# Larger weight transfers over more of the expert loop of a mixture-of-experts decoder layer

## The chip, the cores and the metric

One NeuronCore of a Trainium2 chip (trn2) runs the whole layer. The metric is device time in microseconds (us) of one execution. All data are float32.

## What is computed

One decoder layer over 256 tokens of width 1024: a mixer (a matrix-memory group and an attention group side by side), then a mixture of 32 experts of which each token takes 4, then a gate with per-layer embeddings. The expert part holds nearly all of the bytes: each expert has an up matrix of 1024 x 2048 (8 MB) and a down matrix of 1024 x 1024 (4 MB), so 32 experts are 384 MB that are read once.

```python
logits = (t @ w_router + b_router)
top_vals, top_idx = lax.top_k(logits, TOP_K)
wts = jax.nn.softmax(top_vals, axis=-1)
...
for e in range(N_EXPERTS):
    hu = t @ w_gu[e] + b_gu[e]
    glu = jnp.minimum(hu[:, :D_FF], SWIGLU_LIMIT)
    lin = jnp.clip(hu[:, D_FF:], -SWIGLU_LIMIT, SWIGLU_LIMIT)
    act = glu * jax.nn.sigmoid(SWIGLU_ALPHA * glu) * (lin + 1.0)
    y = y + gates[:, e:e + 1] * (act @ w_dn[e] + b_dn[e])
```

## The kernel before

**Stages.** TensorE (PE) first computes the mixer, up to about 165 us of the trace, then the experts in 16 pairs (pair 0 to 15), then the last gate from about 1069 us on. Up to 64 tokens of each expert are gathered, multiplied with the expert's weights and scattered back; with these inputs one pass of the pair loop suffices.

**Positions.** Expert weights come in chunks of 2 MB (128 partitions x 4096 numbers): four for an expert's up matrix, two for its down matrix, so 12 a pair. `STREAM` gives their order within a pair: four up chunks of the even expert, two up chunks of the odd one, the even expert's two down chunks, the odd one's other two up chunks, its two down chunks. The last pair uses `LAST_STREAM`: all eight up chunks, then the four down chunks. The chunks of all pairs in this order are the positions 0 to 192 (`AT`); one of them, position 150 in pair 12, holds the embedding weights instead. Pair p (up to 12) begins at position 12 p, so pair 1 at 12, pair 2 at 24, pair 4 at 48; pair 15 begins at 181. Two more, 193 and 194, are the weights of the final gate.

**The ring.** A chunk lives in one of ten slots of 2 MB in SBUF (`ring`); an eleventh place, slot 10, is used once. `SLOT_OF[n]` is the slot of position n, picked by the loop at lines 100 to 109: the slot whose last occupant is the oldest. Positions with `FIRST_DOUBLE <= pair < END_DOUBLE` are planned two at a time: a pair of neighbouring slots (0 and 1, 2 and 3, ...) is filled by one transfer of 4 MB, and the pair is picked whose later occupant is the oldest. `FIRST_OF[n]` is the position at which the transfer that brings n begins.

**Loads and releases.** All weight loads are issued by SyncE (SP), in order of position, from one instruction stream. `refill` (line 554 on) waits on the counter `chunk_done` until PE has finished the occupant of the slot (`wait_released`), for a 4 MB transfer until it has finished the later of the two occupants; then `load_position` issues one DMA: line 539 for 2 MB, line 527 for 4 MB.

```python
elif m + 1 < POSITIONS and FIRST_OF[m + 1] == m:
    wait_released(sp, ps, max(occupant(m), occupant(m + 1)))
else:
    wait_released(sp, ps, occupant(m))
load_position(m)
```

PE takes the positions in the same order: `up_chunk` (16 matmuls of line 1129) and `down_chunk` (16 of line 1159) each begin with `wait_position`, which waits for the landing of the transfer that brought the position, so for both halves of a 4 MB one. Between them lie the gathers (line 1072), scatters (line 1080), transposes (1136, 1149) and biases (1121). The last positions, 189 to 192, are loaded and used in parts (lines 531 to 550).

Of the kernel before, what the change touches and what calls it, by code (L numbers as in the profile page):

```python
# [33 lines left out]
def hybrid_layer(nc, x, p, mix_norm_g, w_in, conv_w, conv_b, igate_b, fgate_b, mlstm_head_g, q_norm_g,  # L34
# [10 lines left out]
    PAIRS = E // 2  # L45
# [13 lines left out]
    PRE_SLOT = [4, 6, 8, 0, 1, 2, 4, 6, 8]  # L59
    MOE_SLOT = list(range(RING))  # L60
    HT_SLOT, CONST_SLOT, GATE_SLOT, V_SLOT, OUT_SLOT, MIX_SLOT = 3, 5, 6, 7, 8, 9
    FIRST_DOUBLE, END_DOUBLE = 4, 15
    LATE = 16 * 7
    GATE_STEPS = 10
    POST = 7
# [7 lines left out]
    POSITIONS = PER_PASS + 1  # L73
# [14 lines left out]
    AT = CHUNKS[:PLE_AT] + [None] + CHUNKS[PLE_AT:]  # L88
# [3 lines left out]
    def last_in(slot):  # L92

        return max(i for i, held in enumerate(SLOT_OF) if held == slot)

    def usable(slot):

        return slot != X_SLOT and (len(SLOT_OF) <= PLE_AT or slot != SLOT_OF[PLE_AT])

    while len(SLOT_OF) < POSITIONS + FINALS:  # L100
        n = len(SLOT_OF)
        if n < POSITIONS and AT[n] is not None and FIRST_DOUBLE <= AT[n][0] < END_DOUBLE:
            assert AT[n][:3] == AT[n + 1][:3] and AT[n][3] % 2 == 0 and AT[n + 1][3] == AT[n][3] + 1
            low = min((s for s in range(0, X_SLOT, 2) if usable(s) and usable(s + 1)), key=lambda s: max(last_in(s), last_in(s + 1)))
            SLOT_OF += [low, low + 1]
            FIRST_OF += [n, n]
        else:
            SLOT_OF.append(min((s for s in range(X_SLOT) if usable(s)), key=last_in))
            FIRST_OF.append(n)
# [2020 lines left out]
```

## Time and profile before

| | us |
|---|---|
| median of 3 runs | 1104.46 |
| lowest and highest of them | 1103.58, 1105.56 |
| the profiled execution, its own time | 1103.95 |
| its span in the trace | 1101.7 |
| PE busy, share of the span | 1072.8, 97% |
| bytes read from HBM | 430.04 MB, 391 GB/s over the span |

The span is what the trace covers; 2.3 us of the execution's time lie around it. A landing is the moment at which all 16 DMA engines have finished their part of a transfer. The profile gives it as the time from the issue on SP.

### The profile page before, as it was taken

What the parts mean: (1) busy time and instruction counts of PE and PEld (TensorE: products, weight loads), DVE (VectorE), ACT (ScalarE), POOL (GpSimd) and SP (SyncE); (2) the same over time, 40 slices, a digit from 0 to 9 for tenths busy, and PEclk for the clock granted to TensorE, in tenths of its full rate; (3) what the DMA queues carried; (4) which work ended last, traced back from release to release, by engine and by line L of the source; (5) the groups of instructions that cost most, each with busy time, mean ns of one, the idle gap of its engine ahead of it and who ended that gap; (6) DMA issues with size and microseconds to landing.
All of it is one profiled execution on the core that took longest, in us unless ns stands there. A gap on an engine that the chain in (4) does not pass through costs nothing.

```text
span 1101.7 us, 11963 instructions
## 1 busy us (share of the span) xinstructions
PE 1072.8 (97%) x5130; PEld 448.5 (41%) x5130; DVE 258.4 (23%) x531; ACT 144.6 (13%) x283; POOL 17.3 (2%) x45
## 2 busy tenths in 40 slices
PE   9999999999999999999998989898989899999998
PEld 5485563434343434343433333333333243534334
DVE  4274232231111212121211111121111011211122
ACT  4134341100000000000000000000000110000022
POOL 2001200000000000000000000000000000000000
PEclk9999999999999999999999999999999899999999
DMA  9943589999999999999999999999999999999981
GB/s 348 365 170 114 239 349 396 427 406 428 427 428 434 428 432 433 429 429 432 432 429 430 432 431 428 434 429 434 431 428 430 432 429 431 431 430 425 422 358 39
DMA packets 33787, 431.87 MB, mean 392 GB/s; under 512 B 5207, under 2 KB 5727, under 8 KB 16582
## 3 DMA queue, kind: packets, MB, share of 16 engines
q1 hardware_dynamic: 33520, 431.06, 92.9%
q8 instruction: 41, 0.67, 0.2%
q14 instruction: 12, 0.10, 0.0%
q10 hardware_dynamic: 214, 0.04, 0.0%
HBM read 430.04 MB, written 1.06 MB: 391 GB/s over the span
## 4 chain that ended last, share of the span: by engine, by line
PE 78%; DMA 21%; DVE 0%; issue 0%; ACT 0%; DVEq 0%; ACTq 0%
PE hu L1129 29%; DMA ring<-in_w_gate_up 17%; PE po L1159 17%; PE aux L1072 5%; PE hu L752 5%; PE aux L1080 3%; DMA ring<-in_w_down 3%; PE hu L758 3%; PE hu L1121 2%; PE hu L768 2%; PE po L1136 1%; PE hu L794 1%; PE aux L1340 1%; PE aux L1105 1%; PE hu L1159 1%; PE po L1340 1%
## 5 line engine op out<-in xcount | busy, mean ns | idle before, releaser
L1129 PE MATMUL hu<-ring,num_xg 128*64 128x512 f32 x1920 | 435.1, 600 | 16.8 <-DMA ring<-in_w_gate_up 16.6
L1129 PEld LDWEIGHTS hu<-ring,num_xg 128*64 128x64 f32 x1920 | 132.1, 137 | 299.8 <-issue 273.0
L1159 PE MATMUL po<-ring,arena 128*64 128x512 f32 x976 | 219.2, 601 | 6.2 <-DMA ring<-in_w_down 6.2
L1159 PEld LDWEIGHTS po<-ring,arena 128*64 128x64 f32 x976 | 70.4, 138 | 149.8 <-issue 146.4
L1711 DVE TENSOR_SCALAR arena<-hu 128x512 f32<-128x512 f32 x31 | 21.4, 692 | 426.0 <-PE hu L1129 426.0
L1687 DVE TENSOR_TENSOR arena<-arena,aux 128x512 f32<-128x512 f32 x58 | 37.3, 684 | 133.7 <-PE aux L1080 121.9
L1072 PEld LDWEIGHTS aux<-num_xg,big 128*128 128x128 f32 x512 | 58.4, 192 | 13.0 <-issue 13.0
L1072 PE MATMUL aux<-num_xg,big 128*128 128x128 f32 x512 | 61.4, 278 | 0.0
L752 PE MATMUL hu<-ring 128*128 128x512 f32 x128 | 56.7, 595 | 0.0
L1700 DVE TENSOR_SCALAR arena<-iota_s,posm,gates 128x128 f32<-128x128 f32 x64 | 17.9, 342 | 118.2 <-PE po L1159 115.3
L2034 ACT ACTIVATE hu<-arena 128x512 f32<-128x512 f32 x31 | 18.6, 601 | 194.4 <-DVE arena L1711 194.4
L2050 ACT COPY arena<-po 128x512 f32<-128x512 f32 x16 | 9.4, 585 | 223.2 <-PE po L1149 223.2
L1080 PE MATMUL aux<-num_xg,arena 64*128 64x512 f32 x124 | 35.0, 641 | 0.1
L752 PEld LDWEIGHTS hu<-ring 128*128 128x128 f32 x128 | 23.8, 190 | 27.7 <-issue 27.4
L1121 PE MATMUL hu<-bias,sel_part 32*64 32x512 f32 x256 | 34.8, 612 | 0.0
L1080 PE MATMUL aux<-arena 64*128 64x512 f32 x124 | 31.8, 589 | 0.0
L2042 ACT COPY num_xg<-po 128x512 f32<-128x512 f32 x16 | 9.4, 585 | 158.7 <-PE po L1159 158.7
L2038 ACT COPY arena<-po 128x512 f32<-128x512 f32 x31 | 18.1, 585 | 91.1 <-PE po L1136 91.1
L758 PE MATMUL hu<-ring 128*128 128x256 f32 x128 | 29.5, 385 | 0.0
L1129 PE MATMUL hu<-ring,arena 128*64 128x512 f32 x128 | 28.3, 595 | 0.1
L758 PEld LDWEIGHTS hu<-ring 128*128 128x128 f32 x128 | 23.7, 190 | 4.8 <-DVE ring L1490 1.0
L768 PE MATMUL hu<-ring 128*128 128x512 f32 (+1 forms) x64 | 25.5, 542 | 0.0
(275 smaller groups left out, 607.0 us busy)
## 6 DMA issues: line engine op xcount, KB each, us to landing
ring<-in_w_gate_up SPq DMA_DIRECT2D x44, 4096.0 KB, 35.3
ring<-in_w_down SPq DMA_DIRECT2D x22, 4096.0 KB, 35.7
ring<-in_w_gate_up SPq DMA_DIRECT2D x37, 2048.0 KB, 15.2
ring<-in_w_down SPq DMA_DIRECT2D x14, 2048.0 KB, 16.6
ring<-in_w_in SPq DMA_DIRECT2D x6, 2048.0 KB, 16.2
ring<-in_w_down SPq DMA_DIRECT2D x8, 1024.0 KB, 32.5
ring<-in_w_gate_up SPq DMA_DIRECT2D x6, 1024.0 KB, 7.0
ring<-in_w_out SPq DMA_DIRECT2D x2, 2048.0 KB, 11.3
```

Source lines behind the costliest of these rows:

```text
L752: last = mm(bank, hT[:, k, tt * P:(tt + 1) * P], slot(n, NB, K)[:, k, :], start=(k == 0), stop=(k == K - 1))
L758: last = mm(bank[:, 0:S], slot(n, NB, K)[:, k, ct * P:(ct + 1) * P], hT[:, k, :], start=(k == 0), stop=(k == K - 1))
L768: last = mm(bank[:, lo:hi], mixT[:, k, tt * P:(tt + 1) * P], slot(n, D, 4)[:, k % 4, b * NB + lo:b * NB + hi], start=(k == 4), stop=(k == 3))
L1072: last = mm(bank[:, (k % 4) * P:(k % 4 + 1) * P], h2[:, tt, k * P:(k + 1) * P], onehot[:, tt, :, :].rearrange("p e s -> p (e s)"), start=( ...
L1080: return mm(bank, ghotT[r, e, tt * P:(tt + 1) * P], out_s[e][r, :], start=(e == 0), stop=(e == 1 and not more))
L1121: mm(hu[n * SLOTS:(n + 1) * SLOTS, 2 * e + b, :], expert_rows(b, expert), features(bias[32 * b:32 * b + E, :], n), start=first, stop=False ...
L1129: last = mm(hu[n * SLOTS:(n + 1) * SLOTS, 2 * e + b, :], rows_of[:, k, e * SLOTS:(e + 1) * SLOTS], features(w[:, o:o + D], n), start=first ...
L1159: last = mm(bank[n * SLOTS:(n + 1) * SLOTS, :], actT[:, f, h * SLOTS:(h + 1) * SLOTS], w[:, o:o + NB], start=(h == 0 and f == 0), stop=(h ...
L1340: last = mm(fin_bank(q, lo, hi), x3T[:, k, tt * P:(tt + 1) * P], final_slot(k // 4, D, 4)[:, k % 4, n * NB + lo:n * NB + hi], start=(k == ...
L1687: v.tensor_tensor(quad(xt, q), quad(xt, q), banks[q], ALU.add).then_inc(y_done, 1)
L1711: v.tensor_scalar(glu, hu[:, 2 * e, :], LIMIT, None, ALU.min).then_inc(glu_ready, 1)
L2034: a.activation(hu[:, 2 * e, :], gated(2 * pair + e), ACT.Sigmoid, scale=ALPHA).then_inc(sig_ready, 1)
```

## The change

`FIRST_DOUBLE` is 2 instead of 4, `END_DOUBLE` goes, and of pair 15 the up chunks (kind 0) are planned two at a time as well. The down chunks of pair 15 stay single.

```diff
-    FIRST_DOUBLE, END_DOUBLE = 4, 15
+    FIRST_DOUBLE = 2
...
-        if n < POSITIONS and AT[n] is not None and FIRST_DOUBLE <= AT[n][0] < END_DOUBLE:
+        if n < POSITIONS and AT[n] is not None and FIRST_DOUBLE <= AT[n][0] and AT[n][:2] != (PAIRS - 1, 1):
             assert AT[n][:3] == AT[n + 1][:3] and AT[n][3] % 2 == 0 and AT[n + 1][3] == AT[n][3] + 1
             low = min((s for s in range(0, X_SLOT, 2) if usable(s) and usable(s + 1)), key=lambda s: max(last_in(s), last_in(s + 1)))
             SLOT_OF += [low, low + 1]
```

So 24 transfers of 2 MB in pairs 2 and 3 become 12 of 4 MB, and 8 in pair 15 become 4. The plan that the rule gives, for the places where a load's release changes (the number is the position that PE must have finished before the load is issued):

| load of | before: slot, waits for | after: slots, wait for |
|---|---|---|
| 24 / 25 | 3, 14 / 4, 15 | 4 and 5, 16 |
| 26 / 27 | 5, 16 / 6, 17 | 6 and 7, 18 |
| 28 / 29 | 7, 18 / 8, 19 | 8 and 9, 20 |
| 30 / 31 | 9, 20 / 0, 21 | 0 and 1, 22 |
| 46 / 47 | 5, 36 / 6, 37 | 6 and 7, 37 |
| 48 / 49 | 8 and 9, 40 | 8 and 9, 39 |
| 50 / 51 | 0 and 1, 42 | 0 and 1, 41 |
| 52 / 53 | 2 and 3, 44 | 2 and 3, 43 |
| 54 / 55 | 4 and 5, 46 | 4 and 5, 45 |
| 56 / 57 up to 179 / 180 | the same | the same |
| 181 / 182 | 1, 141 / 8, 173 | 8 and 9, 174 |
| 183 / 184 | 9, 174 / 2, 175 | 2 and 3, 176 |
| 185 / 186 | 3, 176 / 4, 177 | 4 and 5, 178 |
| 187 / 188 | 5, 178 / 6, 179 | 6 and 7, 180 |
| 189 | 7, 180 | 1, 141 |
| 193, 194 | 2, 184; 3, 185 | 3, 184; 4, 185 |

On SP, in pairs 1 and 2, the instruction stream before has these rows (line, what, shape, what it waits for, how many in a row). The first four rows are positions 13 to 23, the x6 row is 24 to 29 of pair 2, the last row its 30 and 31:

```order
L539 DMA ring<-in_w_gate_up 128x4096 [waits chunk_done] x5
L539 DMA ring<-in_w_down 128x4096 [waits chunk_done] x2
L539 DMA ring<-in_w_gate_up 128x4096 [waits chunk_done] x2
L539 DMA ring<-in_w_down 128x4096 [waits chunk_done] x2
L539 DMA ring<-in_w_gate_up 128x4096 [waits chunk_done] x6
L539 DMA ring<-in_w_down 128x4096 [waits chunk_done] x2
```

And now:

```order
L539 DMA ring<-in_w_gate_up 128x4096 [waits chunk_done] x5
L539 DMA ring<-in_w_down 128x4096 [waits chunk_done] x2
L539 DMA ring<-in_w_gate_up 128x4096 [waits chunk_done] x2
L539 DMA ring<-in_w_down 128x4096 [waits chunk_done] x2
L527 DMA ring<-in_w_gate_up 128x8192 [waits chunk_done] x3
L527 DMA ring<-in_w_down 128x8192 [waits chunk_done]
```

The six loads of positions 24 to 29 have become three of twice the size, the two of 30 and 31 one; nothing ahead of them moved.

On SP at the turn from pair 14 to pair 15, before (the first three rows are the last loads of pair 14, the x8 row the up chunks of pair 15):

```order
L527 DMA ring<-in_w_down 128x8192
L527 DMA ring<-in_w_gate_up 128x8192
L527 DMA ring<-in_w_down 128x8192
L539 DMA ring<-in_w_gate_up 128x4096 x8
L531 DMA ring<-in_w_down 128x2048
```

And now:

```order
L527 DMA ring<-in_w_down 128x8192
L527 DMA ring<-in_w_gate_up 128x8192
L527 DMA ring<-in_w_down 128x8192
L527 DMA ring<-in_w_gate_up 128x8192 x4
L531 DMA ring<-in_w_down 128x2048
```

Eight loads have become four; the down chunks behind them are loaded in the same parts as before. The matmuls of PE keep their order in all pairs; only what each waits for changes.

## Rows read from the trace of the kernel before

**Rows 1.** the page's slices of the span: GB/s in 40 slices of 27.5 us

```profile
GB/s 348 365 170 114 239 349 396 427 406 428 427 428 434 428 432 433 429 429 432 432 429 430 432 431 428 434 429 434 431 428 430 432 429 431 431 430 425 422 358 39
```

**Rows 2.** chain that ended last, in order of time: start us, us, what

```profile
340.72 7.02 PE hu L1129 x32
...
394.06 7.02 PE hu L1129 x32
...
542.89 38.94 DMA ring<-in_w_gate_up
...
1060.12 5.30 PE hu L1159 x24
1069.39 7.05 PE aux L1340 x16
```

**Rows 3.** busy time by stretch; the last three columns: PE clock, DMA share, GB/s

```profile
core 0: us, PE busy (x) PEld busy (x) DVE busy (x) ACT busy (x) POOL busy (x), PEclk, DMA share, GB/s
190.00:245.00 55.00, 54.92 (x280) 21.23 (x278) 16.15 (x27) 5.08 (x9) 0.00 (x0) 1.00 1.00 417
245.00:347.00 102.00, 102.00 (x514) 38.82 (x512) 21.13 (x38) 7.67 (x13) 0.00 (x0) 1.00 1.01 428
347.00:540.00 193.00, 193.00 (x972) 74.26 (x970) 37.07 (x65) 14.74 (x25) 0.00 (x0) 1.00 1.01 432
540.00:870.00 330.00, 306.96 (x1492) 113.02 (x1490) 60.01 (x108) 23.58 (x40) 0.00 (x0) 0.99 1.00 431
870.00:981.00 111.00, 111.00 (x539) 43.77 (x537) 20.59 (x38) 9.41 (x16) 0.00 (x0) 0.98 1.00 431
981.00:1045.00 64.00, 64.00 (x324) 23.92 (x322) 12.80 (x22) 5.31 (x9) 0.00 (x0) 1.00 1.00 425
```

**Rows 4.** timeline of PE in pair 1, positions 15, 16 and 18, 19: start us, us, what

```profile
233.98 7.09 PE L1129 MATMUL hu<-ring,num_xg 128*64 128x512 f32 x32
...
246.18 7.04 PE L1159 MATMUL po<-ring,arena 128*64 128x512 f32 x32
```

**Rows 5.** timeline of SP, its DMA issues, 215 to 260 us: start us, us, what

```profile
222.35 5.83 SPq L539 DMA_DIRECT2D ring<-in_w_down  x2
233.50 20.08 SPq L539 DMA_DIRECT2D ring<-in_w_gate_up  x6
```

**Rows 6.** line 539, the issue of position 23 and that of position 25, with landing

```profile
L539 SPq DMA_DIRECT2D ring<-in_w_down x1: 328/328/328, 227.9 to 227.9; - x1
...
DMA to landing us min/median/max: 9.4/9.4/9.4
...
L539 SPq DMA_DIRECT2D ring<-in_w_gate_up x1: 328/328/328, 237.7 to 237.7; - x1
...
DMA to landing us min/median/max: 11.2/11.2/11.2
```

**Rows 7.** DMA before an issue into an empty queue, and that issue's landing

```profile
100.00:106.50 6.50, 6.50 (x18) 2.63 (x16) 0.51 (x3) 2.10 (x3) 1.41 (x2) 1.00 0.00 0
...
L539 SPq DMA_DIRECT2D ring<-in_w_gate_up x1: 327/327/327, 106.5 to 106.5; - x1
...
DMA to landing us min/median/max: 7.1/7.1/7.1
```

**Rows 8.** timeline of PE in pair 15, positions 184, 185 and 186 to 188

```profile
1030.42 7.09 PE L1129 MATMUL hu<-ring,num_xg 128*64 128x512 f32 x32
...
1039.13 10.52 PE L1129 MATMUL hu<-ring,num_xg 128*64 128x512 f32 x48
```

**Rows 9.** line 539, the issue of position 186 and that of position 188, with landing

```profile
L539 SPq DMA_DIRECT2D ring<-in_w_gate_up x1: 328/328/328, 999.8 to 999.8; - x1
...
DMA to landing us min/median/max: 34.7/34.7/34.7
...
L539 SPq DMA_DIRECT2D ring<-in_w_gate_up x1: 328/328/328, 1012.1 to 1012.1; - x1
...
DMA to landing us min/median/max: 32.2/32.2/32.2
```

## The prediction

> **What bounds the kernel now.** I read the busy time by stretch first. TensorE (PE) is busy all the time in every stretch but the one from 540 to 870 us, where it stands for 330.00 - 306.96 = 23.0 us [rows 3]. That looks like a kernel bound by PE with a small hole. The last two columns of the same rows say otherwise: from 190 us on the DMA share is 1.00 and the rate 425 to 432 GB/s in every full stretch, and the page's slices show that it stays there up to some 30 us before the end [rows 1, 3]. Next the chain that ended last, for the pace of each. The same group of matmuls starts at 340.72 and at 394.06, so PE needs 53.3 us for a pair [rows 2]. A pair's weights are 12 x 2.097 MB = 25.2 MB, at 431 GB/s 58.4 us. DMA is thus 5 us a pair slower than PE; PE lives off its stock in the ring, which is used up at 543 us, where the chain goes over to DMA [rows 2]. **From 190 us on the last byte of the weights comes when the DMA engines have moved them all, and a microsecond in which they have nothing queued is given back nowhere**, whoever is waiting at that moment. PE has slack at 240 us, by the two paces some 303 / 53.3 x 5.1 = 29 us, and that slack does not help: to spend it sooner only brings the first stall forward.
>
> In the last pair the two are level. PE does not stand between 870 and 1045 us [rows 3], and from there its chain runs through to the final gate at 1069.39 [rows 2].
>
> **The change, part 1: the first load of pair 2 is issued later.** Here the ring is full and SP waits for PE. Before, position 24 (2 MB) is issued at 233.50, when PE is through with position 14 [rows 5]. Position 23, the last one ahead of it, is issued at 227.9 and lands 9.4 later, at 237.3 [rows 6]. So the queue is fed 3.8 us before it would run dry. Now 24 and 25 come in one transfer that needs slots 4 and 5, and so waits for position 16. PE is through with 15 and 16 at 233.98 + 7.09 = 241.1 [rows 4]. From 237.3 to 241.1 nothing is queued.
>
> What a start from an empty queue costs can be read where the trace has one. In 100 to 106.5 us the DMA share is 0.00, then a 2 MB load is issued at 106.5 and lands 7.1 us later [rows 7]. The second 2 MB of the new transfer follow at 431 GB/s, 4.9 us. It lands at 241.1 + 7.1 + 4.9 = 253.1. Before, position 25 was there at 237.7 + 11.2 = 248.9 [rows 6]. **Cost: +4.2 us.** It can't be less than with no start time at all, 241.1 + 9.7 = 250.8, which is +1.9. It can be more: before, 23 to 25 took 248.9 - 237.3 = 11.6 us, where the pace is 9.8 for 4 MB, though the queue was not empty, only short [rows 6]. If a short queue costs these 1.8 us, the next load may cost them again: 26 and 27 wait for position 18, which ends at 246.18 + 3.5 = 249.7 [rows 4], 3.4 us ahead of 253.1. So the bounds are +1.9 and +6.0, and I take +4.2, since both its parts are measured and 1.8 us in one place may be an accident of that place. The later loads of pairs 2 and 3 also wait for a position closer to their own, 8 or 9 back instead of 10, but each pair DMA falls 5 us further behind PE, so that slots come free well before DMA gets to them.
>
> **Part 2: the rate.** With 2 MB transfers the rate is 428 GB/s (245 to 347 us), with 4 MB transfers 431 and 432 [rows 3]. 4.194 MB take 9.80 us at 428 and 9.73 at 431. The other 11 transfers of pairs 2 and 3 give 11 x 0.07 = **-0.8 us**; the ends are 0 (rounding of the rate) and -1.0 (at 432). The 16 issues fewer on SP, 0.33 us each [rows 6], give nothing: SP mostly waits between them [rows 5].
>
> **Part 3: the up chunks of pair 15.** PE now waits for both halves before it begins the first. Before, 185 begins at 1030.42 + 3.5 = 1033.9 [rows 8], and its other half, 186, lands at 999.8 + 34.7 = 1034.5 [rows 9]. 187 begins at 1039.13 + 10.52 / 3 = 1042.6 (the second third of 48 matmuls) [rows 8], and 188 lands at 1012.1 + 32.2 = 1044.3 [rows 9]. Four larger transfers at the better rate bring this forward by 4 x 0.07 = 0.3, to 1044.0. PE thus begins 187 at 1044.0 instead of 1042.6, +1.4. Behind it PE was not waiting for data in any way that could absorb this: it goes through positions 189 to 192 and the scatters in one piece up to 1069.39 [rows 2]. **Cost: +1.4 us**, between +1.0 and +1.7 (without the rate). The later issues of these loads cost nothing: before, they lay 30 us and more between issue and landing [rows 9], so issues 5 to 9 us later still find a queue.
>
> At this place a rule of the pages speaks for the change. The row shows what a start costs when it is alone: 7.1 us for 2 MB, of which 4.9 are bytes [rows 7], and the rates show that back to back two transfers cost 0.07 us more than one of twice the size [rows 3]. The Trainium skill, "DMA: Bandwidth & Descriptors", section "Anatomy of one DMA", puts a DMA at about 2.0 us plus its bytes at 436 GB/s; that is 6.8 us for 2 MB, near the 7.1 of the trace. Charged to every transfer it would make 16 transfers fewer worth 32 us. The rival that follows from it is below.
>
> **The sum.** 4.2 - 0.8 + 1.4 = +4.8 us. The profiled execution took 1103.95, the median is 1104.46, half a microsecond above it; I set the base between them at 1104.2 and come to **1109.0 us**, slower by 0.4%.
>
> **The rivals.**
> - *A short queue costs again* (chance 0.15). The 1.8 us of [rows 6] come back at the loads of 26 or 30, which are again issued 3 to 4 us before the queue is dry: 1109.0 + 1.8 = 1110.8, twice 1112.6. For it speaks the one place where the trace has a short queue; against it that this is one place.
> - *The dry moment is not on the path* (0.08). If PE's pace set the end, the 4.2 us would vanish in the 29 us of slack, and a little of part 3 would be left: about 1104 to 1105. Against it stand the DMA share of 1.00 over 850 us and the 23.0 us that PE stands [rows 3].
> - *Fewer transfers are worth more than the rate shows* (0.03, the faster side). Place: the queue of SP's loads. Each transfer would bear a part x of the 7.1 - 4.9 = 2.2 us that a start costs alone, also when the queue is full. 16 transfers fewer against 4.2 + 1.4 = 5.6 us: it decides from x = 0.35 us on. With the whole 2.2 us it would be 1104.2 + 5.6 - 35 = 1075. Against it: with x = 0.35 the rate of 4 MB transfers would have to be 444 GB/s against 428, and it is 431 to 432 [rows 3]. By the page's 2.0 us it would be 1078.
>
> That the change does not do what it says is ruled out by the order of SP's loads: 16 more issues of 4 MB, 32 fewer of 2 MB.
>
> **How the numbers follow.** The forecast has 0.74. What a measurement of this kernel can tell from no change is 0.2%, 2.2 us, so up to 1106.7. The low end is the sum of the lower bounds, 1.9 - 1.0 + 1.0 = +1.9, 1106.1; the high end takes in the first rival once and part of the second time, 1111.5. Range **1106.2 to 1111.5**. Slower by over 0.2%: 0.87 (forecast and first rival, less the low end of the forecast). Within 0.2%: 0.10. Faster: 0.03.
>
> **What would show it.** In the changed kernel's slices the GB/s of 220 to 248 us falls from 406 to about 350. SP issues the first 4 MB load at 241.1, DMA is idle from 237 to about 242, and the load lands 12 us after its issue. From pair 4 to pair 14 every landing is some 3.4 us later than before, PE's first wait on weights comes a little before 543 us, and its idle time between 540 and 870 grows from 23.0 by 3 to 4 us. In pair 15 PE waits before positions 185 and 187, 1.4 us together, and ends 4.8 us later. If DMA is never idle near 240 us, or the landings of pairs 5 to 14 are where they were, part 1 is wrong; if PE begins 189 with data long landed and no wait in pair 15, part 3 is.

## The result and the profile after

| | us |
|---|---|
| before, median of the runs compared | 1104.07 |
| changed, median of 4 runs | 1109.84 (1109.4 to 1112.2) |
| ratio, changed to before | 1.0056, 95% interval 1.0044 to 1.0068 |
| span in the trace, before and changed | 1101.7, 1107.2 |

The change costs 5.8 us by the medians; by the ratio it is 0.56%, and its interval stands for 4.9 to 7.5 us. The forecast was 1109.0, with a range of 1106.2 to 1111.5, so it held. First the busy time by stretch of the changed kernel, with one more stretch around 240 us (columns as in [rows 3]; the last two are DMA share and GB/s):

```profile
235.00:242.00 7.00, 7.00 (x38) 2.35 (x34) 2.67 (x4) 1.19 (x2) 0.00 (x0) 1.00 0.24 75
190.00:245.00 55.00, 54.92 (x278) 21.18 (x276) 16.14 (x27) 5.08 (x9) 0.00 (x0) 1.00 0.90 375
245.00:347.00 102.00, 102.00 (x512) 38.64 (x508) 21.32 (x38) 7.67 (x13) 0.00 (x0) 1.00 1.00 431
347.00:540.00 193.00, 189.04 (x952) 73.10 (x952) 36.87 (x64) 14.74 (x25) 0.00 (x0) 1.00 1.00 431
540.00:870.00 330.00, 310.04 (x1504) 113.71 (x1502) 60.02 (x108) 23.58 (x40) 0.00 (x0) 0.98 1.00 431
870.00:981.00 111.00, 109.19 (x530) 43.28 (x532) 20.36 (x37) 9.41 (x16) 0.00 (x0) 0.98 1.00 431
981.00:1045.00 64.00, 62.86 (x316) 23.26 (x314) 13.01 (x22) 5.31 (x9) 0.00 (x0) 1.00 1.00 429
```

Read the DMA share first. Between 235 and 242 us it is 0.24, so a DMA engine stands there for 7.00 x 0.76 = 5.3 us on average; the row of 190 to 245 holds the same hole (0.90), and every other stretch has 1.00. The packets say the same: the last ends at 236.2, the next begins at 241.5. PE is busy all through that stretch: at the place where the time is lost, the engine that looks busiest shows nothing. PE shows it later, and in more than one row: 4.0 us idle in 347 to 540, 20.0 in 540 to 870, 1.8 and 1.1 after 870, together 26.9 where before it was 23.0 [rows 3]. The slices of the page tell the same (the ninth is 220 to 248 us before, with 406 GB/s [rows 1], and 221 to 249 us in this trace, with 318):

```profile
GB/s 349 365 164 127 243 351 395 426 318 435 431 430 429 430 434 431 427 434 429 430 430 432 433 430 430 430 433 430 428 431 429 434 428 430 434 429 432 419 342 38
```

SP's timeline shows why. The first row below holds the issues of positions 22 and 23, the latter at 227.3; then nothing is issued until 240.5:

```profile
221.79 5.83 SPq L539 DMA_DIRECT2D ring<-in_w_down  x2
240.54 15.91 SPq L527 DMA_DIRECT2D ring<-in_w_gate_up  x3
```

The issue of the first 4 MB load (24 and 25) with its landing, and below it that of 28 and 29:

```profile
L527 SPq DMA_DIRECT2D ring<-in_w_gate_up x1: 328/328/328, 240.5 to 240.5; - x1
...
DMA to landing us min/median/max: 12.4/12.4/12.4
...
L527 SPq DMA_DIRECT2D ring<-in_w_gate_up x1: 327/327/327, 256.1 to 256.1; - x1
...
DMA to landing us min/median/max: 17.2/17.2/17.2
```

Positions 24 and 25 are there at 240.5 + 12.4 = 252.9, where before 25 came at 248.9 [rows 6]. The two traces are not quite in step: at 234 us PE is 0.56 us earlier in this one. Against PE's work the delay is 4.6 us. Below, "set in step" means that PE's start of position 14 is laid on that of the kernel before.

At the other end, the chain of the changed kernel, in order of time:

```profile
1018.81 29.13 DMA ring<-in_w_gate_up
...
1047.98 7.09 PE hu L1129 x32
...
1065.55 5.30 PE hu L1159 x24
...
1074.81 7.06 PE aux L1340 x16
```

Position 187 begins when 188 has landed, at 1047.98 instead of 1042.6 [rows 8]. The last two rows answer to 1060.12 and 1069.39 of before [rows 2]; both are 5.4 us later, so nothing is won or lost behind position 187. Landings alone are less late there: 188 comes at 1047.9 instead of 1044.3 [rows 9], +3.7 with the second decimal. The rest, 1.7, is what PE lost by waiting for a second half.

### The profile page after: what moved, and what is told of

Its sections match the earlier page's. It is cut to its first block, busy times and chain, and to the rows that moved or that the text cites. A ratio compares the mean times of both kernels' runs of the same rounds, so it can differ in the third digit from the quotient of the medians.

```text
span 1107.2 us, 11953 instructions
## 1 busy us (share of the span) xinstructions
PE 1073.6 (97%) x5130; PEld 447.5 (40%) x5130; DVE 258.4 (23%) x531; ACT 144.6 (13%) x283; POOL 17.3 (2%) x45
## 4 chain that ended last, share of the span: by engine, by line
PE 70%; DMA 29%; DVE 0%; issue 0%; ACT 0%; SPq 0%; DVEq 0%; ACTq 0%
DMA ring<-in_w_gate_up 26%; PE hu L1129 24%; PE po L1159 15%; PE aux L1072 5%; PE hu L752 5%; DMA ring<-in_w_down 3%; PE hu L758 3%; PE aux L1080 2%; PE hu L768 2%; PE hu L1121 2%; PE hu L794 1%; PE aux L1340 1%; PE po L1136 1%; PE aux L1105 1%; PE hu L1159 1%; PE po L1340 1%
## 6 DMA issues: line engine op xcount, KB each, us to landing
ring<-in_w_out SPq DMA_DIRECT2D x2, 2048.0 KB, 12.1
```

## The experiments

Theory: the queue of DMA runs dry once, because a 4 MB load has to wait for the later of two slots, and the last pair costs PE a wait for a second half. Rival 1: only the last pair costs. Rival 2: larger transfers cost something each. Each run is compared with runs of the kernel before on the same chip (median 1103.87 for the first four, 1103.71 for the last three).

### Pairs 2 and 3 alone

```diff
-    FIRST_DOUBLE, END_DOUBLE = 4, 15
+    FIRST_DOUBLE, END_DOUBLE = 2, 15
```

> Pairs 2 and 3 in 4 MB transfers, pair 15 as before. Theory (the DMA queue runs dry while SP waits for position 16): the first 4 MB load is issued at 241 us, DMA stands some 5 us, position 24/25 lands 12 us after the issue, all later landings are 4.0 to 4.6 us later than before up to the end, and the time is +4.0 to +4.6 against before: 1108.1 to 1108.7. Rival 1 (the last pair's larger loads are what costs, the early gap lies in the slack of PE): 1104.0 +- 0.7, the same as before. Rival 2 (4 MB transfers as such cost something each): also slower, but with the loss spread over the 12 transfers and not in one place.

Measured: 1108.55, ratio 1.0044 (1.0030 to 1.0058), +4.7 us, just above the 4.0 to 4.6 expected. Its stretch around 240 us:

```profile
235.00:242.00 7.00, 7.00 (x38) 2.53 (x38) 2.67 (x4) 0.81 (x2) 0.00 (x0) 1.00 0.15 61
```

The first load is issued at 241.1 and lands 12.6 us later. With the two traces set in step by PE's start of position 14, the landings are later than before by 4.8 us at position 25, 5.7 at 29, 5.0 at 47, 5.1 at 149 and 5.1 at 192. The loss arises at 25, grows by 0.9 at 29, falls back by 0.7 up to 47 and then stays to the end. Rival 1 falls.

### The last pair alone

```diff
-    FIRST_DOUBLE, END_DOUBLE = 4, 15
+    FIRST_DOUBLE = 4
...
-        if n < POSITIONS and AT[n] is not None and FIRST_DOUBLE <= AT[n][0] < END_DOUBLE:
+        if n < POSITIONS and AT[n] is not None and FIRST_DOUBLE <= AT[n][0] and AT[n][:2] != (PAIRS - 1, 1):
```

> Only pair 15's up chunks in 4 MB transfers, pairs 2 and 3 as before. Theory (PE waits for the second half before it begins the first): PE waits before 185 and 187, 1.4 us together, landings of 182 to 188 0.0 to 0.3 us earlier than before, time +1.0 to +1.7: 1105.1 to 1105.8. Rival 1 of the run of pairs 2 and 3: +5.5 here. Rival 3 (fewer transfers pay in the last pair): 1103.7 or less, and PE begins 189 no later than before.

Measured: 1105.37, ratio 1.0013 (1.0003 to 1.0022), +1.5 us. Its chain:

```profile
1016.94 27.46 DMA ring<-in_w_gate_up
...
1044.44 7.09 PE hu L1129 x32
...
1071.26 7.05 PE aux L1340 x16
```

As in the changed kernel position 187 waits for 188; the gate starts 1.9 us later than before [rows 2]. Together with the run before, 4.7 + 1.5 = 6.2, against 5.8 for the whole change. The two parts add up within what the runs vary.

### The later issue alone, no larger transfer

```diff
                 else:
-                    wait_released(sp, ps, occupant(m))
+                    wait_released(sp, ps, 16 if m == 24 else occupant(m))
                 load_position(m)
```

> The kernel before, all transfers of their old size, but SP waits for position 16 instead of 14 before it issues the 2 MB load of position 24. Theory: the later issue alone costs what the change costs at pair 2: position 25 lands at 241.1 + 7.1 + 4.9 = 253.1 instead of 248.9, and the time is +4.0 to +4.6: 1108.1 to 1108.7. Rival 2 (the size of the transfers costs, not the moment of the issue): same as before, 1104.1 +- 0.7.

Measured: 1108.92, ratio 1.0049 (1.0035 to 1.0063), +5.1 us, where 4.0 to 4.6 was expected. The stretch around 240 us, and the load of position 24:

```profile
235.00:242.00 7.00, 7.00 (x38) 2.35 (x34) 2.67 (x4) 1.19 (x2) 0.00 (x0) 1.00 0.22 56
```

```profile
L539 SPq DMA_DIRECT2D ring<-in_w_gate_up x1: 328/328/328, 240.6 to 240.6; - x1
...
DMA to landing us min/median/max: 7.6/7.6/7.6
```

No transfer has another size than before, and the loss is the whole loss of pairs 2 and 3 (4.7). This is the run that settles part 1: one wait of SP, 7 us longer than before (240.6 instead of 233.5), costs 5 us at the end of the kernel, 860 us later. Rival 2 is not needed.

### Larger transfers that wait less

```diff
-    FIRST_DOUBLE, END_DOUBLE = 4, 15
+    FIRST_DOUBLE = 2
...
-        if n < POSITIONS and AT[n] is not None and FIRST_DOUBLE <= AT[n][0] < END_DOUBLE:
+        if n < POSITIONS and AT[n] is not None and FIRST_DOUBLE <= AT[n][0] < PAIRS - 1 and n not in (30, 31, 32, 33):
...
-            low = min((s for s in range(0, X_SLOT, 2) if usable(s) and usable(s + 1)), key=lambda s: max(last_in(s), last_in(s + 1)))
+            low = min((s for s in range(n < 30, X_SLOT - 1, 2) if usable(s) and usable(s + 1)), key=lambda s: max(last_in(s), last_in(s + 1)))
```

> 4 MB transfers from pair 2 on, but those of 24, 26 and 28 go to slots 3 and 4, 5 and 6, 7 and 8, so that they wait for positions 15, 17 and 19 instead of 16, 18 and 20; 30 to 33 in 2 MB transfers; pair 15 as before. Theory: the first 4 MB load is issued at 237.7, 3.4 us earlier than in the changed kernel, DMA stands about 1 us instead of 5, position 25 lands at 237.7 + 12.3 = 250.0 instead of 248.9, and the time is +0.5 to +1.3: 1104.6 to 1105.4. Rival 2 (size): 9 of the 12 transfers are still larger, so 3/4 of the loss of pairs 2 and 3 stays, +3.2.

Measured: 1105.77, ratio 1.0018 (1.0009 to 1.0027), +1.9 us: most of the loss is gone, but more is left than expected. The stretch around 240 us shows 7.00 x 0.35 = 2.5 us of standing DMA, not 1:

```profile
235.00:242.00 7.00, 7.00 (x40) 2.49 (x36) 2.68 (x4) 1.02 (x2) 0.00 (x0) 1.00 0.65 246
```

The 1 left out the start: the last packet ends at 236.4, the next begins at 238.4. The load is issued at 237.5, as forecast, but lands 13.5 us later and not 12.3; why it takes 1.1 us more than the same load of the changed kernel (12.4) is open. Set in step, position 25 lands 2.3 us later than before. Then one more load falls behind. That of positions 34 and 35 is issued at 286.6, 3.3 us ahead of the landing before it, and lands at 301.1, 14.5 us later. That is 11.2 us after that landing, where the pace is 9.7, so 1.5 us are lost. I first took this for the price of a short queue, and the expectation of the run from pair 3 on rests on it. The same trace speaks against it. Positions 68 and 69 are issued 24.4 us ahead of the landing before theirs (456.6), with a deep queue, and land 11.3 us after it:

```profile
L527 SPq DMA_DIRECT2D ring<-in_w_gate_up x1: 328/328/328, 432.2 to 432.2; - x1
...
DMA to landing us min/median/max: 35.7/35.7/35.7
```

Such steps return all through every trace; the last section has them.

### The start of the larger transfers moved

From position 30 on:

```diff
-        if n < POSITIONS and AT[n] is not None and FIRST_DOUBLE <= AT[n][0] < END_DOUBLE:
+        if n < POSITIONS and AT[n] is not None and 30 <= n and AT[n][0] < END_DOUBLE:
```

> 4 MB transfers from position 30 on (9 of the 12 of pairs 2 and 3), pair 15 as before. Theory: the load of 30 and 31 waits for position 22, which PE ends at 268.9; it is issued just as position 29 lands (268.5), so that DMA runs dry once, here. By the run with odd slots, where an issue 0.7 us behind the last landing cost 4.5 us, the landings from 31 on are 3.2 to 4.5 us later and those up to 29 unchanged; time +3.2 to +4.5. Rival (a loss per larger transfer): also +3.5, but the landings fall behind step by step from 31 to 47.

Measured: 1107.39, ratio 1.0032 (1.0020 to 1.0044), +3.7 us, as expected. DMA is busy around 240 us and stands around 268 us, half of 6 us:

```profile
235.00:242.00 7.00, 7.00 (x40) 2.49 (x36) 2.67 (x4) 1.03 (x2) 0.00 (x0) 1.00 1.00 403
266.00:272.00 6.00, 6.00 (x32) 2.00 (x30) 0.00 (x0) 0.00 (x0) 0.00 (x0) 1.00 0.50 167
```

The place of the loss moves with the place of the late issue, as the theory has it. Set in step with before, landings are level at 29 (+0.1), +2.8 at 31, +4.2 at 33 and +3.4 from 47 on. 2.8 of it arises at the late issue, 1.4 at position 32, a step as above. From 33 on it does not grow, so the rival of a loss per transfer falls, though its time is the same.

From pair 3 on:

```diff
-    FIRST_DOUBLE, END_DOUBLE = 4, 15
+    FIRST_DOUBLE, END_DOUBLE = 3, 15
```

> 4 MB transfers from pair 3 (position 36) on, pair 15 as before. Theory: the load of 36 and 37 waits for position 28, which ends 3.4 us ahead of the landing of 35; the queue doesn't run dry but is short, which cost 1.5 us in the odd slots run and nothing at position 26 of the changed kernel. So landings from 37 on +0 to +1.5, time 0 to +1.5. Rival (a loss per larger transfer, 6 of 12): +2.3.

Measured: 1104.20, ratio 1.0000 (0.9991 to 1.0010), no difference; the rival had +2.3 and falls. The load of 36 and 37, issued only 3.0 us ahead of the landing before it, lost nothing. That of 38 and 39, issued at 302.7, 4.0 us ahead, lost 1.8, again a step that returns in this trace with a deep queue (1.5 at positions 80, 124 and 169).

From position 40 on, and of pair 15 only 181 to 184:

```diff
-        if n < POSITIONS and AT[n] is not None and FIRST_DOUBLE <= AT[n][0] < END_DOUBLE:
+        if n < POSITIONS and AT[n] is not None and (40 <= n and AT[n][0] < END_DOUBLE or 181 <= n < 185):
```

> Larger transfers only where neither cost can arise: from position 40 on, where each load is issued 5 us or more ahead of the landing before it, and in pair 15 only for 181 to 184, whose second halves land before PE needs the first. 185 to 188 stay in 2 MB. Theory: no landing is later than before, the rate gives 6 x 0.07 us, time -0.4 +- 0.7, no difference that can be measured. Rival (a loss per larger transfer, 4 of 12 and 2 of 4): +2.2.

Measured: 1103.22, ratio 0.9994 (0.9985 to 1.0003), -0.5 us. The rival of a loss per larger transfer had +2.2 and falls here too. It is the lowest median of all these kernels, and it is not shown to be faster than before: the interval holds 1. What the larger transfers have to give in this kernel is of that size.

## Why the prediction was right, point by point

**The bound.** That DMA's work ends the kernel, and that PE's slack in the middle does not cover a dry moment, was the step on which all else rested. The run with the later issue alone shows it: PE does the same work with the same transfers and the time is 5.1 us longer. One row was misread on the way: 542.89 in [rows 2] is the issue of a load that lands 38.94 us later, at 581.8, and not the moment at which the stock is used up. PE's first wait on weights, 0.2 us, is at 543.0 all the same, and the longer ones (2.6 us) begin at 581.9. The rival "the dry moment is not on the path" is out.

**Part 1, the late issue** (forecast +4.2). Measured by the landing of 24 and 25 it is +4.6 against PE's work. The issue came where it was forecast (240.5, in step 241.1), and the price was near: 12.4 us from issue to landing, where 7.1 + 4.9 = 12.0 was worked out from the trace of before. There is luck in the other side of the subtraction. The 248.9 at which position 25 landed before holds 1.9 us of a step (11.7 us for 23 to 25, where the pace is 9.8). In the four other traces whose kernels are unchanged up to there, it lands between 0.9 earlier and 0.5 later than that, set in step; from the trace of the start at 30 (248.0 in step) the same working would have given +5.1.

**Part 2, the rate** (forecast -0.8). The price of one transfer was right, the sum was not. The GB/s did rise as forecast, from 428 to 431 in 245 to 347 us. Where no step disturbs them, two loads of 2 MB take 9.78 us (before, position 30 to 43: 273.39 to 336.99) and one of 4 MB 9.71 (changed, 33 to 47: 292.88 to 360.86), 0.07 less, as forecast. But the landing of 46 and 47 follows that of 24 and 25 by 108.0 us in the changed kernel (252.9 to 334.1 + 26.8) and by 108.0 before (248.9 to 356.9). With the same late issue and 2 MB transfers it takes 108.6 (253.12 to 361.73, against 252.91 to 360.86), so the larger transfers do give 0.7 us. One step takes it back, 28 and 29, which land 10.7 us after 26 and 27 instead of 9.7. The prediction had no term for such steps. The kernel before has one too, but at 24 and 25, just ahead of the 108.0 us. The run of the later issue alone and that of pairs 2 and 3 alone have theirs at 28, as the changed kernel; that with odd slots, whose queue also runs dry at 24, has none there. So no run shows that the dry moment or the larger transfers make the step. The sum should have been +4.6 + 0.0 for pairs 2 and 3; the run with them alone has +4.7.

**Part 3, the last pair** (forecast +1.4). Alone +1.5. In the changed kernel PE is 5.4 us late where landings are 3.7 late, so 1.7, which counts the 0.3 us that the landings gained since position 180: 1.4 against their old pace.

**The sum.** +4.8 was forecast, +5.8 measured (4.9 to 7.5). The terms as measured are 4.6 + 0.0 + 1.4 = 6.0: 0.8 more than forecast by the rate term and 0.4 by part 1, less what the runs vary.

**The first rival**, a short queue that costs again, did not come true: 26 and 27, issued 3.7 us ahead, followed at the pace of 9.7. As a mechanism it is not shown either. Its one witness was the 1.8 us of [rows 6], and the same trace loses 1.2 us at positions 64, 108 and 153, which are issued 21 to 30 us ahead.

**The third rival**, fewer transfers that are worth more than the rate shows, is out: 16 fewer, and the time is 5.8 us longer; 6 fewer (the run from position 40 on), and it is within 0.15% of before. The 2.0 us that the prediction takes from the Trainium skill, "DMA: Bandwidth & Descriptors", section "Anatomy of one DMA", are fitted there to transfers that GpSimd issues; here SP issues them. A charge like it shows in a load that starts alone (7.1 to 7.6 us for 2 MB), and back to back only 0.07 us of it.

**What the profile was to show.** Right: the issue at 241, the standing DMA, the landing after 12 us, and PE's waits before 185 and 187 (0.5 + 0.8 = 1.3 us, forecast 1.4). Wrong in size: I expected GB/s of about 350 in the ninth slice, it is 318. The 350 counts only the 3.8 us from the landing of 23 to the issue; DMA stood 5.3, since the first packet comes 1.0 us after the issue and the engines end at different times before the landing. Wrong in size too: the landings of pairs 4 to 14 are mostly 4.5 to 4.8 us later in step (3.7 to 5.1), not 3.4. Wrong in place: PE's idle time in 540 to 870 us was to grow by 3 to 4 us; it fell to 20.0, while 4.0 appear between 347 and 540. PE's row of waits on weights begins at 508 us instead of 543: the stock is smaller by 4.6 us and shrinks by only 5.1 us a pair, so the first stall moves by a good part of a pair, not "a little". It is no sharp measure, though: with the last pair alone changed, so the same kernel up to there, it begins at 524. The total, 26.9 against 23.0, grew by what was expected.

## What to carry to other kernels

Where the DMA share is 1.00 over most of the span, look at the few places where its queue is shortest, however busy the compute engine is there: an issue that comes 3 to 4 us after the last landing was paid in full at the end here, with the start on top (+4.7 and +5.1 us in the two runs that have nothing else). Before two transfers are joined, write down what each waited for; the joined one waits for the later, and it is ready only when its second half is. So join them where the queue is deep and the second half has landed before the first is needed, and leave them single elsewhere. Before a loss behind a short queue is put down to the queue, look for the same loss where the queue is deep. And at 2 MB already, joining gives little: two rates of a stretch, 428 and 431 GB/s, said so beforehand.

## What the runs showed of the hardware

- **Single loads fall behind again and again, with a deep queue as with a short one.** Loads of 2 MB land 4.9 us apart, of 4 MB 9.7, but in every trace a step of about 0.9 to 1.8 us (in some traces two smaller ones near each other) returns some 34 to 47 positions after the last. The loads from position 64 on in this table were issued 12 to 32 us ahead of the landing before them:

| kernel | position: us lost against the pace |
|---|---|
| before | 24 and 25: 1.9; 64: 1.2; 108: 1.2; 153: 1.2 |
| changed | 28: 1.0; 68: 1.0; 112: 1.0; 159: 0.9 |
| odd slots | 34: 1.5; 68: 1.6; 112: 1.4; 159: 1.5 |
| start at 30 | 32: 1.4; 74: 1.2; 118: 1.3; 165: 1.2 |
| start at pair 3 | 38: 1.8; 80: 1.5; 124: 1.5; 169: 1.5 |

  Loads issued 3.0, 3.7 and 4.8 us ahead lost nothing. So a price of a short queue that has not run dry is not shown; what sets the place and the size of a step is open.
- **The 16 DMA engines drift apart, and do so at these steps.** The 16 parts of one transfer land one by one. In the run with odd slots they are 3.0, 4.5, 6.0 and 7.2 us apart at its positions 34, 68, 112 and 159: each step widens the spread by about what the landing loses. In the trace before, the 16 parts of position 23 arrive between 235.5 and 237.2, those of position 192 between 1056.6 and 1064.2. A transfer is as late as its slowest part, and at the end that is 7.6 us behind the fastest. Behind the dry moment of the changed kernel the parts of 24 and 25 arrive within 252.1 to 252.9; it sets the engines level again, yet at 192 they lie 6.7 us apart once more.
- **What a dry queue costs.** In the changed kernel the last packet ends at 236.2, 0.3 us before the landing at 236.5. The first packet of the next load begins 1.0 us after its issue (240.5 to 241.5). From an issue into an empty queue to the landing it took 7.1 us (2 MB, before) and 7.6 (2 MB, the later issue alone), 12.4 and 12.6 us (4 MB). Loads issued within 1 us of the last landing vary: 8.5 (2 MB, before, issued at 143.8), 13.5 (4 MB, odd slots) and 12.1 (4 MB, start at 30).
